# Three projection granules moved behind the mixers of a hybrid encoder layer, with the conversions and memsets around them

## What is computed

```python
xn = rmsnorm(x, norm_mix)
p = xn @ w_in                                  # 2048 -> 6400
pA, pB, pC, pD = jnp.split(p, [A_COLS, A_COLS + B_COLS, A_COLS + B_COLS + C_COLS], axis=-1)
yA = rwkv7_mixer(pA, ...)                      # 8 heads of 64, a state that runs over the frames
yB = chunk_band_attention(qB, kB, vB, band_rel_bias)        # 8 heads of 64
yC = diff_attention(qC, kC, vC, t5_rel_bias, lam, ...)      # 4 heads of 2 x 64
yD = short_conv_mixer(pD, conv_w)              # b * conv3(c * h), 512 channels
x = x + jnp.concatenate([yA, yB, yC, yD], -1) @ w_out
x = x + hier_moe(rmsnorm(x, norm_ffn), ...)    # 4 groups of 8 experts of width 256, all weights read
return rmsnorm(x, norm_final)
```

## Time and profile before

| | |
|---|---|
| Time, median of 3 runs | 1014.21 us (1012.27 to 1014.83) |
| Profiled execution | 1014.21 us, of which the span from first to last instruction 1012.3 us |
| TensorE busy | 975.9 us (96%) |
| VectorE busy | 451.3 us (45%) |
| ScalarE busy | 275.2 us (27%) |
| GpSimd busy | 74.1 us (7%) |
| TensorE's clock, mean share granted | 0.991 |

### The profile page before, as it was taken

One profiled execution on the slowest core, in us unless ns is written; L12 is line 12 of the kernel. 1 busy time (PEld: TensorE's weight loads), 2 busy tenths in 40 slices (PEclk: granted clock), 3 DMA queues, 4 the chain that ended last, 5 costly groups with the idle time before them and its releaser, 6 DMA issues.

```text
span 1012.3 us, 18314 instructions
## 1 busy us (share of the span) xinstructions
PE 975.9 (96%) x8119; PEld 750.6 (74%) x8119; DVE 451.3 (45%) x699; ACT 275.2 (27%) x445; POOL 74.1 (7%) x81
## 2 busy tenths in 40 slices
PE   5999899999998999999999999999999999999995
PEld 4999899998998999978888656556565656566542
DVE  4648957444456557675435024141323223141404
ACT  4455343232224556634541000010001000000103
POOL 5010002214010000240000000000000000000000
PEclk9999899999999999999999999999999999999998
DMA  9685454222424443679959899999999999999992
GB/s 272 187 253 166 125 160 133 86 86 85 126 86 128 138 149 127 224 246 357 365 182 387 358 421 431 427 427 427 427 427 428 426 428 427 428 428 426 425 378 89
DMA packets 83459, 285.81 MB, mean 282 GB/s; under 512 B 5756, under 2 KB 57032, under 8 KB 70960
## 3 DMA queue, kind: packets, MB, share of 16 engines
q1 hardware_dynamic: 79344, 279.98, 71.8%
q0 software_dynamic: 1824, 4.04, 1.5%
q10 hardware_dynamic: 2208, 0.57, 0.3%
HBM read 280.36 MB, written 4.22 MB: 281 GB/s over the span
## 4 chain that ended last, share of the span: by engine, by line
PE 89%; DVE 5%; DMA 2%; POOL 2%; issue 1%; ACT 1%; DVEq 0%; ACTq 0%; POOLq 0%
PE bank L916 24%; PE bank L1309 22%; PE bank L1330 10%; PE bank L1282 6%; PE bank L933 3%; PE bank L935 3%; PE bank L934 3%; PE bank L859 2%; PE bank L1291 2%; DMA arena<-in_norm_mix 2%; PE bank L1343 1%; PE bank L1292 1%; PE bank L1032 1%; PE bank L1209 1%; DVE ring_r L1499 1%
## 5 line engine op out<-in xcount | busy, mean ns | idle before, releaser
L916 PE MATMUL bank<-xTr,hi 128*128 128x256 f32 x1344 | 250.2, 287 | 4.4 <-DVE ring_r L1499 4.4
L1309 PE MATMUL bank<-arena 128*64 128x256 f32 x2048 | 232.0, 381 | 1.0 <-DVE arena L1904 1.0
L1499 DVE TENSOR_TENSOR ring_r<-arena,hi 128x1024 fp32r<-128x1024 f32 x132 | 164.5, 1258 | 132.8 <-ACT hi L593 130.8
L916 PEld LDWEIGHTS bank<-xTr,hi 128*128 128x128 f32 x1344 | 212.6, 193 | 9.6 <-DVE ring_r L1499 5.0
L1309 PEld LDWEIGHTS bank<-arena 128*64 128x64 f32 x2048 | 144.6, 137 | 81.5 <-issue 14.2
L916 PE MATMUL bank<-xTr,ring_r 128*128 128x256 f32 x672 | 191.1, 284 | 0.0
L593 ACT ACTIVATE hi<-arena 128x1024 fp32r<-128x1024 f32 x132 | 139.2, 1060 | 128.9 <-PE bank L916 99.1
L916 PEld LDWEIGHTS bank<-xTr,ring_r 128*128 128x128 f32 x672 | 129.9, 193 | 0.0
L1330 PE MATMUL bank<-arena,const 128*64 128x512 f32 x448 | 100.8, 597 | 0.0
L1900 DVE TENSOR_TENSOR arena<-arena,bank 128x512 f32<-128x512 f32 x60 | 63.9, 1110 | 40.6 <-PE bank L1292 40.6
L1330 PEld LDWEIGHTS bank<-arena,const 128*64 128x64 f32 x448 | 30.3, 137 | 54.5 <-issue 52.0
(11 more groups left out here) (314 smaller groups left out, 969.0 us busy)
## 6 DMA issues: line engine op xcount, KB each, us to landing
arena<-in_expert_w_gate SPq DMA_DIRECT2D x32, 2048.0 KB, 21.5
arena<-in_expert_w_up SPq DMA_DIRECT2D x32, 2048.0 KB, 20.8
arena<-in_expert_w_down SPq DMA_DIRECT2D x26, 2048.0 KB, 21.6
arena<-in_w_in SPq DMA_DIRECT2D x50, 1024.0 KB, 5.3
arena<-in_w_out SPq DMA_DIRECT2D x16, 1024.0 KB, 5.9
arena<-in_expert_w_down SPq DMA_DIRECT2D x12, 1024.0 KB, 20.3
arena<-in_x SPq DMA_DIRECT2D x2, 1024.0 KB, 8.1
arena<-in_x SPq DMA_DIRECT2D x4, 512.0 KB, 7.5
```

The costliest lines, as they stand in the source:

```text
L916: ins = MM(PJ[n % 2][:, h * U:(h + 1) * U], a, b, start=False, stop=h == 1 and q == 3 and tt == 3 and k == 2)
L1309: ins = MM(bank[2 + st_][CAP * a:CAP * a + CAP, c // 2 * U:(c // 2 + 1) * U], xg[:, t, CAP * a:CAP * a + CAP], slot(b + a)[:, t * U:(t + 1 ...
L1499: TT(ring_r[:, n % 2, q, :], ring[:, n % 2, q, :], hi[:, g % NHI, :].bitcast(f32), ALU.subtract).then_inc(s["lo_done"], 1)
```

## The change

Three granules are taken out of TensorE's mixer stage: two in front of the doubling loop, one behind the chunk loop. Since the last call runs whatever is left of the input, they come at the end of the attention. ScalarE's `advance` calls and VectorE's `split_lo` calls follow. Beyond that,

- VectorE does one low part behind each half of X and XT, in place of four behind both, and the low parts around the chunk loop are shared out differently: two in its last step, one in place of two under the variance, one in place of three behind the low parts of yA;
- the memsets of the state S move from turns 1 and 2 of the doubling loop to its front, the bias memsets from the first two chunk steps to turns 4 and 5 of the doubling loop;
- at the end of the attention ScalarE's high part of the convolution's first half moves in front of the last `advance`, VectorE's low part of it in front of the low parts 100 to 102 and of VectorE's own convolution;
- in ScalarE's loop over the last four heads `advance(2)` moves behind the exponentials;
- SyncE's loads of the residual x into `x2b` wait for the low part of the last attention head (`ylo_done` at `YC`) in place of the last maximum.

```diff
@@ SyncE
                 if n == NU_IN:
-                    sp.wait_ge(s["sm_done"], sm_count(NBH + NCH - 1))
+                    sp.wait_ge(s["ylo_done"], YC)
@@ ScalarE
-            advance(6)
+            advance(4)
             for i in range(10):
...
                 copy(Gs[rows], K[c // 2][rows, :].rearrange("p (h v) -> p h v", h=8), s["gs_ev"])
                 advance(3)
-            advance(2)
+            advance(1)
...
             for i in range(NCH):
-                advance(2)
                 if i + 1 < NCH:
                     exps(NBH + i + 1)
+                advance(2)
                 probs_copy(NBH + i)
...
-            advance(NG_IN - pos["pe"] + 1)
             act.wait_ge(s["dconv0"], 1)
             copy(yTr[:, 0, 12:14, :], Dq[:, 0, 1], s["yhi_done"])
+            advance(NG_IN - pos["pe"] + 1)
             act.wait_ge(s["dconv1"], 1)
@@ TensorE
-            granules(2)
             for i in range(10):
                 t1(i)
...
                 granules(1)
-            granules(2)
+            granules(1)
             pe.wait_ge(s["ynat_done"], 2)
@@ VectorE
                 step(TT(XT[:, e], XT[:, e], over8(ident64), ALU.add), s["n_ev"])
-            split_lo(4)
+                split_lo(1)
+            v.wait_ge(rel_st, 32)
+            for t in S:
+                step(V.memset(t, 0.0), s["halves_zero"])
             for i in range(10):
...
                 split_lo(1)
-                if i == 1:
-                    v.wait_ge(rel_st, 32)
-                if i in (1, 2):
-                    step(V.memset(S[i - 1], 0.0), s["halves_zero"])
                 if i == 3:
...
+                    v.wait_ge(bias_ld, 64)
+                if 4 <= i < 6:
+                    t = biasB if i == 4 else biasC
+                    step(V.memset(t[CH:P, :, CH:P], NEG))
+                    step(V.memset(t[CH:P, :, P + 3 * CH:3 * P], NEG))
...
                 step(V.tensor_copy(Us[rows], heads(K[4][rows, :])), s["us_ev"])
-                if c < 3:
-                    split_lo(1)
+                split_lo(1)
                 if c == 2:
                     variance(0)
-                if c < 2:
-                    v.wait_ge(bias_ld, 64)
-                    t = (biasB, biasC)[c]
-                    step(V.memset(t[CH:P, :, CH:P], NEG))
-                    step(V.memset(t[CH:P, :, P + 3 * CH:3 * P], NEG))
...
-                if c < 3:
-                    split_lo(1)
+                split_lo(1)
             centre(1)
             variance(1)
-            split_lo(2)
+            split_lo(1)
             scale_gate(1)
...
-            split_lo(3)
+            split_lo(1)
...
             out_low_c(NCH - 1)
+            split_lo(2)
+            v.wait_ge(s["yhi_done"], YD0)
+            step(TT(yTr[:, 1, 12:14, :], Dq[:, 0, 1], yTr[:, 0, 12:14, :].bitcast(f32), ALU.subtract), s["ylo_done"])
             split_lo(NG_IN + LEAD - pos["split"])
             v.wait_ge(s["pj_evac"], NU_IN - NA)
...
             step(TT(c_, c_, b_, ALU.mult), s["dconv1"])
-            v.wait_ge(s["yhi_done"], YD0)
-            step(TT(yTr[:, 1, 12:14, :], Dq[:, 0, 1], yTr[:, 0, 12:14, :].bitcast(f32), ALU.subtract), s["ylo_done"])
             split_lo(1)
```

## The result

The changed kernel took 1031.24 us, the median of four runs from 1030.64 to 1032.56, against 1014.00 us (1012.27 to 1014.83) for the kernel before on the same chip: a ratio of 1.0174, with a 95% interval of 1.0156 to 1.0192. That is +17.2 us by the two medians and +17.6 by the ratio. I had forecast 1025.0 us with a range from 1018.5 to 1029.0: slower, as forecast, but by 17 us where the sum had said 11.

A forecast was written before the change was run, and what follows sets the result against it. TensorE was taken to bound the kernel, mixer idle time reaching the end one for one. The terms 4.0 + 2.8 + 1.8 + 2.9 - 1.9 + 0.2 + 1.0 = +10.8 us on 1014.21 gave 1025.0 us, range 1018.5 to 1029.

The forecast's parts named there:

- What bounds the kernel: Whole kernel: TensorE bounds it, so idle time added or removed in the mixer stage arrives at the end one for one.
- First term: Doubling loop's entry: without two granules, TensorE waits for VectorE's first half of X before t1(0); +4.0 us.
- second term: Doubling loop, before t1(1): lo(43) between the halves of X waits for ScalarE and delays the second half; +2.8 us.
- Third term: Memsets moved before and into the doubling loop delay its adds, less what other turns gain; +1.8 us (0 to 3.0).
- Fourth term: End of the chunk loop: one granule fewer, so TensorE waits before the transposes of Yn; +2.9 us (1.7 to 4.1).
- Fifth term: Attention's entry: fewer VectorE conversions before the softmax shorten TensorE's wait for probabilities; -1.9 us (-2.3 to 0).
- Sixth term: Convolution at the attention's end: waits of 2.0 and 0.5 us replace one of 2.3; +0.2 us (-0.5 to +1.4).
- Seventh term: Clock: the wait at the doubling loop's entry brings a fall to 1.2 GHz; +1.0 us (0 to 2.8).
- (a): Rival, faster: late waits shrink and nothing opens at the doubling loop's entry; 1009.3 us, chance 0.07.
- (b): Rival, no change: idle time only moves, absorbed by a later load or the convolution; 1011.2 to 1017.2 us, chance 0.05.
- (c): Rival: the first wait at the doubling loop's entry comes, but not the second; 1018 to 1022 us, chance 0.12.
- (d): Rival, dearer: low clock over both entry waits and the convolution at its upper bound; about 1028 us, chance 0.10.

The follow-up runs named there:

- b2_fill: The changed kernel with 14 matmuls of no use added ahead of the first t1 and 14 ahead of the transposes of Yn: 1033.41 us, ratio 1.0194.
- a3_halves: The changed kernel, but VectorE builds both halves of X together and does the two low parts behind them: 1030.12 us, ratio 1.0164.
- b1_memsets: The changed kernel with VectorE's memsets and lam operations put in front of the low parts instead of behind them: 1029.64 us, ratio 1.0153.
- a4_conv: The changed kernel with the convolution's order on ScalarE and VectorE put back as before: 1029.63 us, ratio 1.0161.
- a1_noswap: The changed kernel with only the swap of `exps` and `advance(2)` in ScalarE's loop over the last four heads undone: 1023.96 us, ratio 1.0108.
- a2_swap_alone: The kernel before with nothing but the swap of `exps` and `advance(2)` in ScalarE's loop over the last four heads: 1019.24 us, ratio 1.0059.
- c1_entry: The changed kernel with two granules, two ScalarE high parts and four VectorE low parts put back before the doubling loop: 1029.46 us, ratio 1.0161.
- the two filled kernels: The changed kernel with 14, or 7, matmuls of no use ahead of the first t1 and of the transposes of Yn: 1033.41 and 1029.25 us.

## Why the prediction was right, and where it was wrong

- **What bounds the kernel: right.** TensorE's idle time in the mixer stage arrives at the end; the expert stage takes up none of it (idle 1.0 before and after).
- **First term and second term: right.** 4.0 and 2.8 forecast, 3.85 and 2.94 measured: t1(0) to t1(1) takes 7.09 us at full clock (167.93 to 175.02 in b2_fill; 7.2 forecast), less 4.15. The changed kernel's 7.91 holds 0.8 of half clock, which I had as a term of its own at 1.0. a3_halves took away the second wait by its named cause alone.
- **Third term, memsets: right**, 1.8 against 2.1 in the trace. The waits where memsets stand are 1.07, 1.09 and 0.57, forecast 0.85, 1.05 and 0.55. The 2.1 of b1_memsets is no second measurement of this term, since that kernel also loses what its turns lost before.
- **Fourth term, end of the chunk loop: 0.8 too small.** GpSimd's power took 2.62 us with one conversion beside it, as with two; I had taken 1.5 from one conversion fewer. The rest was as forecast: VectorE's centre(1) stood 1.37 us behind the end of TensorE's last products (302.51 and 301.14), 0.11 before. The wait was 3.47, the term 3.7.
- **Fifth term: the wait did shrink** by 2.4 (2.65 to 0.24), more than the 1.9, but the half clock behind the 3.47 us took 1.4 of it (9.41 us without the wait, against 8.05 before). I had not carried the fourth term's wait on to the clock.
- **Sixth term: within its bounds for another reason, which is luck.** 0.2 against 1.1: the first wait was 1.83 (2.0 forecast) and the second did not come, as VectorE's convolution took 4.3 us (452.36 to 456.64), not 5.2; the half clock behind it took 1.5.
- **Seventh term, the clock: one fall counted, four came.** Each fall was priced where it stood: 0.8 us over t1(0), 1.5 over the transposes of Yn, nothing at the heads, 1.5 behind the convolution. The first was in the sum; of the others 3.0 us were missing, of which smaller waits than forecast gave back 1.2 (2.4 for 1.9, and at the convolution 1.83 for 2.5). a4_conv saw less of the last 1.5 than the trace has, so that price is the least certain. These are prices of one execution: behind the same wait the transposes of Yn lost 1.5 us here and 2.4 in b1_memsets (10.54 us, 308.75 to 319.29).
- **The step that failed: the swap of `exps` and `advance(2)` had no term.** The part on the attention costed its entry and its end, and took the loop between as neutral. The swap put two conversions behind a wait of 5.86 us on VectorE's row maximum, and so VectorE's low parts, the low part of the head before and the value products behind both: 6.2 us in the trace, 6.7 in a1_noswap, 6.0 in a2_swap_alone. With it the sum is 17.0, against 17.2 to 17.6 measured. That this is so near is in part luck, since the traces' rows add up to 2.9 more than 17.0. That ScalarE's order matters as VectorE's does was in the prediction's own argument on the second wait; the rows of ScalarE's timeline at 380 to 410 in the kernel before would have shown it: there a conversion runs at 394.42 and the exponentials follow at 395.38 with no wait for `nmx` between them.
- **The rivals.** None was this one. (a) and (b) fell with the waits at the entry, (c) with the 2.01 in front of t1(1). (d), dearer by clock and convolution, had the right sign and the wrong place.

What stays open: when a wait is followed by half clock. A wait of 1.83 us in front of 450.09 was followed by half clock in the changed kernel, and one of 1.83 in front of 443.58 in a1_noswap was not (113.91 us for the same stretch, at a clock of 1.00, against 115.47 at 0.99). And c1_entry kept 1.3 us in its times where its trace has 3.1; with intervals of 1.3 us on its ratio and 1.8 on that of the change, the two are compatible.

## What to carry to other kernels

In a static order over several engines, go through the diff line by line and write a term for each moved call, nought included, with the row that covers it: the line that I passed over cost more than any single term that I worked out. Ask of each reordered pair which of the two waits, and for what: independent work belongs in front of the one that waits. And price a repair in the place where it will run, since work held back from one place may be the cover of a later one: of the 7.8 us won from the entry to 310, 1.3 were left in the time.

## What the runs showed of the hardware

- **Half clock has a price only where TensorE sets the pace.** A fall of the clock cost 1.5 us over the transposes of Yn (9.65 against 8.12) and nothing at the heads (13.75 against 13.76). Filling a wait with matmuls of no use kept the clock up over what followed at once, but at the entry the clock fell with the next wait, 2.63 us, just the same.
- **The length of a wait alone did not decide on the fall**: 1.83 us with and without one, 2.65 and 2.29 without, 2.63 and 2.64 with one in the two filled kernels, 3.21 in front of the value products with one in the changed kernel and without in b1_memsets. Nor was its depth fixed: behind the wait of 3.50 us near 120, in code that no edit touches, the clock over the next 11.6 us was 0.74, 0.85 and 1.00 (the kernel before, the changed kernel, b2_fill). A term for the clock is a chance and not a constant.
- **VectorE's convolution took 4.3 us with GpSimd at rest and 6.4 beside it**; the last product on 128x512 took 0.69 and 1.67 us. That agrees with the Trainium skill (GPSIMD Engine Reference, "Key points") on the shared interfaces, as quoted in the prediction. GpSimd's power on 128x8 took 2.62 us with two conversions of VectorE beside it and with one, and 1.67 us in the kernel before at 283.77, where VectorE was idle from 283.62 to 284.86; between one conversion and two its time does not follow their number.
